# Row work between the pieces of each key choice, eight row buffers, and one-hot columns on three engines

## What is computed

```python
def peer_ffn(h, wq, subkeys, u, v):          # h: 512 tokens x 1024
    q = (h @ wq).reshape(B, S, 8, 2, 128)
    sub_scores = einsum('bshpk,hpnk->bshpn', q, subkeys)        # 2 x 128 keys for each of 8 heads
    top_v, top_i = top_k(sub_scores, 16)
    cand = top_v[..., 0, :, None] + top_v[..., 1, None, :]      # 16 x 16 sums
    best_v, best_pos = top_k(cand, 16)
    expert = take_along_axis(top_i[0]*128 + top_i[1], best_pos) # 16 of 16384 experts per head
    gates = softmax(best_v)
    hid = gelu(einsum('tkd,td->tk', u[expert], h)) * gates      # 128 slots (8 heads x 16) per token
    return einsum('tk,tkd->td', hid, v[expert])
```

## Time and profile before

| | |
|---|---|
| time, median of 3 runs | 3541.71 us (3536.84 to 3544.75) |
| profiled execution: its time / its span | 3545.33 us / 3543.4 us |
| PE busy | 2911.7 us (82%) |
| DVE busy | 1707.0 us (48%) |
| POOL busy | 1626.4 us (46%) |
| ACT busy | 832.1 us (23%) |
| chain that ended last, by engine | PE 50%, DVE 17%, DMA 15%, POOL 9%, issue 5%, ACT 3% |

### The profile page before, as it was taken

The page is one execution under the profiler, slowest core; times in us unless marked ns, Lnnn a source line. Parts: engine busy times, 40 slices in busy tenths (PEclk is TensorE's granted clock), DMA queues, the critical chain, the costliest instruction groups (busy, mean ns, idle before and its releaser), DMA issues.

```text
span 3543.4 us, 32601 instructions
## 1 busy us (share of the span) xinstructions
PE 2911.7 (82%) x12374; PEld 2224.3 (63%) x12374; DVE 1707.0 (48%) x3162; ACT 832.1 (23%) x1284; POOL 1626.4 (46%) x1235
## 2 busy tenths in 40 slices
PE   6999996898888799999785679999995799999300
PEld 5756885687776577777664558888884644444100
DVE  2021146631242322220326636777767777666888
ACT  3254243124242333332223122111110000000000
POOL 3412446644352267664222022433448953454675
PEclk9999998999998899999885589999996699999755
DMA  4300321032331145543220022888985068999997
GB/s 133 95 1 20 99 76 49 1 95 78 101 125 48 54 131 151 153 143 101 55 71 1 1 93 89 309 336 328 347 346 211 1 234 324 365 409 409 378 354 282
DMA packets 214893, 584.37 MB, mean 165 GB/s; under 512 B 21825, under 2 KB 46546, under 8 KB 214226
## 3 DMA queue, kind: packets, MB, share of 16 engines
q1 hardware_dynamic: 137296, 301.22, 25.2%
q0 software_dynamic: 74688, 271.61, 20.1%
q10 hardware_dynamic: 2754, 9.46, 0.7%
HBM read 574.35 MB, written 7.86 MB: 164 GB/s over the span
## 4 chain that ended last, share of the span: by engine, by line
PE 50%; DVE 17%; DMA 15%; POOL 9%; issue 5%; ACT 3%; DVEq 0%; ACTq 0%; POOLq 0%
PE ps L1039 13%; PE ps L1040 13%; PE ps L1041 13%; DMA rows<-in_v,expert 8%; DMA rows<-in_u,expert 7%; POOL rows L985 6%; PE ps L1448 2%; PE ps L1102 2%; POOL wlo L891 2%; DVE rows L1956 1%; PE ps L1014 1%; PE ps L1114 1%; PE ps L1089 1%; DVE ps L1975 1%; ACT whi L504 1%
## 5 line engine op out<-in xcount | busy, mean ns | idle before, releaser
L891 POOL TENSOR_TENSOR wlo<-wraw,whi 128x1024 fp32r<-128x1024 f32 x306 | 745.2, 2448 | 1031.2 <-ACT whi L504 1031.1
L504 ACT ACTIVATE whi<-wraw 128x1024 fp32r<-128x1024 f32 x306 | 321.6, 1059 | 1001.0 <-PE ps L1041 976.0
L1039 PE MATMUL ps<-hhi,whi 128*128 128x512 f32 x1096 | 434.7, 397 | 30.9 <-DVE hlo L1527 6.8
L1456 PE MATMUL ps<-stream,hg 128*128 128x512 f32 x1024 | 444.0, 597 | 8.2 <-DMA stream<-in_v 7.4
L1432 PE MATMUL ps<-haff,stream 128*128 128x256 f32 x2048 | 445.2, 381 | 2.2 <-ACT stg L843 2.2
L1040 PE MATMUL ps<-hlo,whi 128*128 128x512 f32 x1096 | 432.0, 394 | 0.0
L1041 PE MATMUL ps<-hhi,wlo 128*128 128x512 f32 x1096 | 431.3, 394 | 0.0
L985 POOL DMA_INDIRECT rows<-in_u,expert x256 | 298.1, 1164 | 280.3 <-DVE hid L1956 172.8
L1432 PEld LDWEIGHTS ps<-haff,stream 128*128 128x128 f32 x2048 | 391.0, 191 | 56.0 <-ACT stg L843 2.4
L985 POOL DMA_INDIRECT rows<-in_v,expert x256 | 267.9, 1047 | 285.4 <-DVE ps L1975 105.5
L1956 DVE CUSTOM_DVE_ANT_0 rows<-rows,h_s 128x1024 f32<-128x1024 f32 x256 | 310.3, 1225 | 151.3 <-DMA rows<-in_u,expert 148.0
(11 more groups left out here) (414 smaller groups left out, 4438.5 us busy)
## 6 DMA issues: line engine op xcount, KB each, us to landing
stream<-in_ut SPq DMA_DIRECT2D x128, 512.0 KB, 6.7
stream<-in_v SPq DMA_DIRECT2D x128, 512.0 KB, 6.8
wraw<-in_w_in SPq DMA_DIRECT2D x96, 512.0 KB, 3.7
wraw<-in_w_ada SPq DMA_DIRECT2D x48, 512.0 KB, 3.8
wraw<-in_w_gu SPq DMA_DIRECT2D x88, 256.0 KB, 3.1
wraw<-in_w_down SPq DMA_DIRECT2D x22, 512.0 KB, 3.6
wraw<-in_w_br_ssm SPq DMA_DIRECT2D x16, 512.0 KB, 3.5
wraw<-in_w_xkv SPq DMA_DIRECT2D x16, 512.0 KB, 3.7
```

Of the source, the lines that this page charges most:

```text
L504: act.activation(whi[:, n % WSLOTS, 0:kn, :], wraw[:, n % WSLOTS, 0:kn, :], ACT.Copy).then_inc(w_hi, 1)
L891: pool.tensor_tensor(wlo[:, n % WSLOTS, 0:kn, :], wraw[:, n % WSLOTS, 0:kn, :], whi[:, n % WSLOTS, 0:kn, :].bitcast(F32), ALU.subtract).th ...
L1039: pe.matmul(dst, lh, rh, start=k == 0, stop=False)
L1456: ins = pe.matmul(ps[:, 2 * i + half, :], hg[:, n, P * i:P * i + P], stream[j][:, 4 * half:4 * half + 4, :], start=n == 0, stop=n == NKEYS ...
```

## The change

- `top_keys` takes a function `between` and calls it at eight places of its chain. For the 24 choices that share their time with rows it is `next_row`, which does the next row of the running block; two choices and their block of 16 rows are so woven into one. `dots` and `weighted_rows` become `next_row`. Choices of tile 1 go into blocks 12 to 15 instead of after blocks 11 to 14.
- `RING` is 8. Room for it: the odd sums move from `vacc` to PSUM banks 6 and 7, the scores to the end of `hg` (`tk_dense`, tiles 2 and 3) and to the place of `hot1` (`tk_last`, tile 1). The results of the `u` stream rotate through banks 0 and 1 alone, and the transposes go to banks 2 and 3. `load_scores(8)` and `(9)` wait for the end of the mixing steps.
- One-hot columns: `hot2` is made by DVE in one operation of 128 x 512; of the four columns of `hot1` DVE makes one, ACT two (a square of the difference, then a relu with the gate as bias and its negative as scale) and POOL one.
- `sum_rows` copies the first sum to SBUF before it adds the second.

```diff
-RING = 6
+RING = 8
-TOP_AFTER = {**{b: 4 + b for b in range(8)}, **{b: 1 + b for b in range(11, 15)}}
+TOP_AFTER = {**{b: 4 + b for b in range(8)}, **{b: b for b in range(12, 16)}}
+HOT_DVE, HOT_ACT, HOT_POOL = (0,), (1, 2), (3,)
...
# ACT
-                act.activation(hg[:, n, :], ps[:, n % 4, 0:ND], ACT.Gelu).then_inc(s("hg_ready"), 1)
+                act.activation(hg[:, n, :], ps[:, n % 2, 0:ND], ACT.Gelu).then_inc(s("hg_ready"), 1)
...
+            link(act.activation(slot_n[:], slot_t[:, 0:2, :], ACT.Copy, scale=-1.0))
+            for b in range(ND // 4):
+                if b >= 2:
+                    act.wait_ge(s("mix_mm"), b - 1)
+                for m in HOT_ACT:
+                    c = 4 * b + m
+                    ins = act.activation(hot1[:, b % 2, m, :], cst[:, C_IOTA:C_IOTA + P], ACT.Square, bias=slot_n[:, 1, c:c + 1])
+                link(ins)
+                for m in HOT_ACT:
+                    c = 4 * b + m
+                    ins = act.activation(hot1[:, b % 2, m, :], hot1[:, b % 2, m, :], ACT.Relu, bias=slot_t[:, 0, c:c + 1], scale=slot_n[:, 0, c:c + 1])
+                ins.then_inc(s("hot1_act"), 1)
...
# POOL
+                if q >= 8:
+                    pool.wait_ge(s("mix_mm"), ND // 4)
+                tk_s = tk_dense if q < 8 else tk_last
...
-                for m in range(4):
-                    ins = pool.tensor_scalar(hot2[:, b % 2, m, :], cst[:, C_IOTA:C_IOTA + P], slot_t[:, 2, 4 * b + m:4 * b + m + 1], None, ALU.is_equal)
-                ins.then_inc(s("hot2_ready"), 1)
+                for m in HOT_POOL:
+                    c = 4 * b + m
+                    ins = pool.tensor_scalar(hot1[:, b % 2, m, :], cst[:, C_IOTA:C_IOTA + P], slot_t[:, 1, c:c + 1], slot_t[:, 0, c:c + 1], ALU.is_equal, ALU.mult)
+                ins.then_inc(s("hot1_pool"), 1)
...
# PE
-                if n >= 4:
-                    pe.wait_ge(s("hg_ready"), n - 3)
+                if n >= 2:
+                    pe.wait_ge(s("hg_ready"), n - 1)
...
-                pe.wait_ge(s("hot1_ready"), b + 1)
-                pe.wait_ge(s("hot2_ready"), b + 1)
+                pe.wait_ge(s("hot_dve"), b + 1)
+                pe.wait_ge(s("hot1_act"), b + 1)
+                pe.wait_ge(s("hot1_pool"), b + 1)
...
# DVE: top_keys; seven more such calls follow, the last one after the one-hot products
+            def top_keys(t, h, between=lambda: None):
...
                 for a2 in range(2):
                     ins = v.max(tv[:, a2, 0:8], src[:, a2, :])
                 link(ins)
+                between()
...
# DVE: rows
+            def next_row():
+                b, k = divmod(rows_done[0], TOPK)
+                rows_done[0] += 1
...
+                v.wait_ge(row_landed[j], 16 * count)
+                v.wait_ge(row_used, TOPK * b + k - 1)
+                acc = row_sums(k % 2)
...
+                    v.scalar_tensor_tensor(acc, rows[j][:], wrow[:, n:n + 1], acc, ALU.mult, ALU.add).then_inc(row_used, 1)
...
-            def first_hot(b):
+            def hots(b):
                 if b >= 2:
                     v.wait_ge(s("mix_mm"), b - 1)
-                for m in range(4):
+                v.tensor_tensor(hot2[:, b % 2], cst[:, C_IOTA:C_IOTA + P].unsqueeze(1).to_broadcast([P, 4, P]),
+                                slot_t[:, 2, 4 * b:4 * b + 4].unsqueeze(2).to_broadcast([P, 4, P]), ALU.is_equal)
+                for m in HOT_DVE:
...
-                link(v.tensor_tensor(h2_s[:, t, :], vacc[:], acc, ALU.add))
+                link(v.tensor_copy(h2_s[:, t, :], row_sums(0)))
+                link(v.tensor_tensor(h2_s[:, t, :], h2_s[:, t, :], row_sums(1), ALU.add))
...
             for b, (kind, t, h) in enumerate(BLOCKS):
-                if kind == "u":
-                    dots(b)
-                else:
-                    weighted_rows(b)
                 if b in TOP_AFTER:
                     q = TOP_AFTER[b]
-                    top_keys(*TOP_ORDER[2 * q])
-                    top_keys(*TOP_ORDER[2 * q + 1])
+                    top_keys(*TOP_ORDER[2 * q], between=next_row)
+                    top_keys(*TOP_ORDER[2 * q + 1], between=next_row)
+                while rows_done[0] < TOPK * (b + 1):
+                    next_row()
```

More of the change, by code:

```diff
@@ L327, in build_program @@
         rows = [at(f"rows{j}", KEEP, 4 * j if j < 2 else 16 + 4 * j, [P, D]) for j in range(RING)]
-        stream = [at(f"stream{j}", KEEP, 40 + 4 * j, [P, KD, P]) for j in range(STREAM)]
-        vacc = at("vacc", KEEP, 56, [P, D])
-        tk_s = at("tk_s", KEEP, 60, [P, 2, 2, 2, NKEYS])
+        stream = [at(f"stream{j}", KEEP, 48 + 4 * j, [P, KD, P]) for j in range(STREAM)]
+        tk_dense = at("tk_dense", HG, 124, [P, 2, 2, 2, NKEYS])
+        tk_last = at("tk_last", KEEP, 8, [P, 2, 2, 2, NKEYS])
         slot_t = at("slot_t", KEEP, 64, [P, 3, ND])
+        slot_n = at("slot_n", CONST, 512 / KB, [P, 2, ND])
         gates_d = at("gates_d", KEEP, 64, [P, 2, SLOTS])
@@ L1003, in gpsimd_program @@
                         for m in range(ND // 4):
-                            second_hot(m)
+                            first_hot(m)
+                        load_scores(8)
+                        load_scores(9)
                     if k == TOPK // 2 and b - 1 in TOP_AFTER and TOP_AFTER[b - 1] - 2 < 12:
                         q = TOP_AFTER[b - 1] - 4 + 2
-                        if q < 12:
+                        if q not in (8, 9) and q < 12:
                             load_scores(q)
@@ L1428, in tensor_program @@
                 pe.wait_ge(landed[j], count)
-                if n >= 4:
-                    pe.wait_ge(s("hg_ready"), n - 3)
+                if n >= 2:
+                    pe.wait_ge(s("hg_ready"), n - 1)
                 for k in range(KD):
-                    ins = pe.matmul(ps[:, n % 4, 0:ND], stream[j][:, k, :], haff2[:, 1, k, :], start=k == 0, stop=k == KD - 1)
+                    ins = pe.matmul(ps[:, n % 2, 0:ND], stream[j][:, k, :], haff2[:, 1, k, :], start=k == 0, stop=k == KD - 1)
                 ins.then_inc(s("u_mm"), 1)
@@ L1948, in top_keys @@
                 v.sem_inc(s("head_done"), 1)
[L1950 to L1954, removed]
-                    v.wait_ge(row_landed[j], 16 * count)
[L1956 to L1965, removed]
-                for k in range(TOPK):
-                    j, count = row_count(b, k)
-                    v.wait_ge(row_landed[j], 16 * count)
-                    acc = vacc[:] if k % 2 else ps[:, 4:6, :].rearrange("p a b -> p (a b)")
-                    w = wrow[:, TOPK * h + k:TOPK * h + k + 1]
-                    v.wait_ge(row_used, TOPK * b + k - 1)
-                    if h == 0 and k < 2:
-                        v.tensor_scalar(acc, rows[j][:], w, None, ALU.mult).then_inc(row_used, 1)
-                    else:
-                        v.scalar_tensor_tensor(acc, rows[j][:], w, acc, ALU.mult, ALU.add).then_inc(row_used, 1)
@@ new lines, in vector_program @@
+            rows_done = [0]
+            def next_row():
+                b, k = divmod(rows_done[0], TOPK)
+                rows_done[0] += 1
+                kind, t, h = BLOCKS[b]
+                c = slice(TOPK * h, TOPK * h + TOPK)
+                n = TOPK * h + k
+                j, count = row_count(b, k)
+                if kind == "u":
+                    v.wait_ge(row_landed[j], 16 * count)
+                    v.tensor_tensor_reduce(rows[j][:], rows[j][:], h2_s[:, t, :], 1.0, 0.0, ALU.mult, ALU.add, hid[:, n:n + 1]).then_inc(row_used, 1)
+                    return
+                if k == 0:
+                    v.wait_ge(s("row_gelu"), PEER_HEADS * t + h + 1)
+                    link(v.reciprocal(grec[:, h:h + 1], gsum[:, h:h + 1]))
+                    link(v.scalar_tensor_tensor(wrow[:, c], gates_g[:, t, c], grec[:, h:h + 1], hidg[:, c], ALU.mult, ALU.mult))
+                v.wait_ge(row_landed[j], 16 * count)
+                v.wait_ge(row_used, TOPK * b + k - 1)
+                acc = row_sums(k % 2)
+                if h == 0 and k < 2:
+                    v.tensor_scalar(acc, rows[j][:], wrow[:, n:n + 1], None, ALU.mult).then_inc(row_used, 1)
+                else:
+                    v.scalar_tensor_tensor(acc, rows[j][:], wrow[:, n:n + 1], acc, ALU.mult, ALU.add).then_inc(row_used, 1)
```

37 lines of the change are left out of this document (18 added, 19 removed).

## The result

The changed kernel takes 3398.02 us (median of 4 runs, 3397.41 to 3401.24) against 3540.74 before, ratio 0.9599 (95% interval 0.9582 to 0.9615): 143 us less. The forecast was 3437 with a range from 3400 to 3480. The sign and the way in which the change works held; the size did not: the time lies 2 us under the range, and the gain is 1.4 times the one forecast. Two terms of the sum were too dear, the mixing step and above all the rows that run alone at the end. The profiled execution took 3397.58 us for a span of 3395.7.

The account below looks back on a forecast made before the run. Rows were taken to set the end (DVE, POOL and DMA in a ring, held up by choices and mixing). Mixing 2669.5 to 2781.5, `v` stream to 3232.5, rows to 3413.5, plus 24 and 1.2: span 3439, forecast 3437 us, range 3400 to 3480.

Parts of the forecast that it names:

- Weaving: Row blocks 0 to 7: two key choices woven with sixteen rows take 38.5 us a block instead of 47.7, floor 36.3.
- The stall on the gates goes: Before the mixing: TensorE's 24 us wait for the scaled gates vanishes; first mixing matmul at 2669.5 instead of about 2707.
- The mixing step: 64 mixing steps: mean 1.75 us each instead of 2.35, a quarter of the time at 2.3, the rest at 1.6.
- Block 11 and the woven blocks behind the mixing: After the mixing: block 11 takes 25 us, then blocks 12 to 15 with choices 4 x 38.5 = 154 us.
- The rows beside the stream: Rows done while the `v` stream runs, until 3232.5: 2.09 us each, 130 rows.
- The rows alone: Rows left after the `v` stream ends: 126 at 1.435 us each, 181 us.
- rival 4: Last rows run faster, 1.25 us instead of 1.435, 23 us less; with mixing steps at 1.6, 3404 us; chance 10%.
- 1 (low clock): TensorE stays at the low clock in the mixing: step 2.3 us, 35 us more, 3472 us; chance 12%.
- 2 (DMA binds): DMA or the gather ring still binds the woven blocks, 45 us each: time 3486 us; chance 7%.
- 5 (table loads): ACT loads tables for square and relu in each mixing step: step 4.07 us, 148 us more, 3585 us; chance 5%.
- 6: Woven rows are always waited for, as if unwoven; only the mixing steps gain: 3503 us; chance 3%.
- 3: DVE and POOL hold each other up in the mixing: step 2.1 us, 22 us more, 3459 us; chance 8%.

Follow-up runs that it names:

- two columns on POOL: The changed kernel with one of ACT's two `hot1` columns given to POOL, which then makes two: 3421.8 us, ratio 0.9661 to before.
- old columns: The changed kernel with one-hot columns as before, `hot2` on POOL, all of `hot1` on DVE, none on ACT: 3449.4 us, ratio 0.9736 to before.

## Why the prediction missed, step by step

- *Weaving*, 36.3 us as the floor and 38.5 taken (the sum before the mixing went by 38): 36.5 measured for tiles 2 and 3. The floor is what happened; DMA carried 391 GB/s, and DVE waited for no row. It changed nothing before the mixing, as the prediction said of anything under 41 us.
- *The stall on the gates goes, the mixing starts at 2669.5*: 2667.4. Right, with one surprise inside: the exponent of the gates and a gelu made DVE wait 14.8 and 13.6 us, where I had counted 5 for the exponent (2609 to 2614.4) and nothing for the gelu, and it cost nothing.
- *Two PSUM banks cost nothing*: right. No matmul of the `u` stream waits for a gelu in the changed kernel.
- *The mixing step* was mis-sized: 1.75 us forecast, (2765.3 - 2667.4)/64 = 1.53 measured, 14 us. The engine limits were right (DVE 1.5 to 1.75); the term that failed is "a quarter of the time at 2.3", 10 of the 14 us, and the rest is 1.50 for 1.6. Only the first four steps ran mostly at the low clock; once at 1.00, it never fell. Rows 9 had shown 1.00 at 62% busy, and the forecast gave that row too little weight.
- *Block 11 and the woven blocks behind the mixing*: 26.1 and 151 us (2791.4 to 2942.4) for 25 and 154.
- *The rows beside the stream*: 137 gathers in 275 us, 2.01 us each, for 2.09.
- *The rows alone* were mis-sized: 121 rows (113 gathers and eight in the ring) in 154 us, 1.27 us each, for 126 at 1.435: 154 us for 181, 27 us, of which 20 come from the pace and 7 from the five rows fewer. This is the larger miss, and it was there as rival 4 with 10%, which is what happened. The argument against it was that POOL's mean issue and DMA's share of 0.96 "both stand near the limit already". POOL's mean of 1.12 was not its own cost (0.94) but contained the hold-up by DVE; in the changed kernel it is 0.96 (108.50/113). And 356 GB/s at a share of 0.96 was not DMA's limit, since the earlier trace rows show 401 at 1.01.
- *The end*: 24.7 us after the last row, for 25.2.

In sum 2 + 14 + 27 = 43 us, all that lies between the forecast span of 3439 and 3395.7. Rival 4 had put faster rows and a step of 1.6 us together and came to 3404; what carried the time below the range was the step of 1.53 instead of 1.6 (4.5 us) and the 2 us at the start of the mixing.

Of the other rivals, 1 (low clock), 2 (DMA binds), 5 (table loads) and 6 did not occur; 3 showed only with two columns on POOL.

## What to carry to other kernels

When one chain is late by a fixed hand-over (here TensorE's end of `u`), count the idle time of the others before it. Time saved there is worth nothing, and work moved into it costs nothing: moving one more block there was worth 15 us. Ask of a mean duration what is mixed into it: POOL's 1.12 us were gathers of 0.94 and gathers that began while DVE had two inputs in SBUF; an accumulator in PSUM took that away for the `v` rows. Parts that each remove the same stall must be taken away together to be weighed.

## What the hardware showed that was not expected

- A gather that begins during a DVE operation with two SBUF inputs ends 0.81 us after that operation and so takes up to 1.9 to 2.0 us instead of 0.94; beside one with one SBUF input it never took over 1.2 (0 of 262 gathers in five kernels).
- TensorE's granted clock stayed at 1.00 through sixty steps with 1.13 us of matmuls in each 1.50 us, and through the last 57 with 1.13 in 1.73. With old columns, at 2.34 us a step, it went up and down, with a mean of 0.71.
- A POOL operation of 128 x 128 took 604 ns with one column operand (compare) and 790 with two (compare, then multiply).
